# Moving the second norm of a hybrid backbone step from the token rows to the gathered expert rows

## The reference

```
h   = modulate(rmsnorm(x, norm_mix), sh1, sc1)
q, k, v, p = split(h @ w_in)
mix = concat(attention(q, k, v), pool_mixer(p)) @ w_out
x1  = x + g1 * mix
h2  = rmsnorm(x1, norm_ffn) * (1 + sc2) + sh2
affin = softmax(h2 @ w_router)            # 16 experts
gates, idx = top_k(affin.T, cap)          # 128 latent rows, 32 context rows per expert
y   = (silu(h2[idx] @ w_gate) * (h2[idx] @ w_up)) @ w_down * gates
out = rmsnorm(x1 + g2 * scatter_add(y, idx), norm_final)
```

## Time and profile before

| | us |
|---|---|
| median of 3 runs | 3756.24 (3752.21 to 3762.21) |
| profiled execution, device time | 3750.03 |
| its span in the trace | 3748.1 |

### The profile page before, as it was taken

How to read it: one execution, slowest core, us unless ns; L and a number is a source line. 1 busy time by engine, 2 the same in 40 slices (tenths; PEclk the granted TensorE clock), 3 DMA queues, 4 the chain that set the end, 5 groups by cost and what they waited for, 6 DMA issues and landing times.

```text
span 3748.1 us, 52148 instructions
## 1 busy us (share of the span) xinstructions
PE 3361.9 (90%) x20987; PEld 3033.8 (81%) x20987; DVE 2121.6 (57%) x2206; ACT 1786.9 (48%) x1933; POOL 524.7 (14%) x581
## 2 busy tenths in 40 slices
PE   5899999997889889996676999999999999999991
PEld 4677777776668777786566999999999999999991
DVE  4634433454543345324675777677767777777774
ACT  5643432554542246213324555555555555555552
POOL 1055045002220023002200000000000000000001
PEclk9999999998999889995787999999999999999995
DMA  7765555586133220522437888888888888888876
GB/s 251 259 225 190 180 186 184 185 287 217 35 135 135 90 77 29 202 101 87 166 107 256 274 262 258 256 271 274 274 268 268 265 273 264 257 255 271 274 240 249
DMA packets 541926, 781.11 MB, mean 208 GB/s; under 512 B 15680, under 2 KB 408944, under 8 KB 529408
## 3 DMA queue, kind: packets, MB, share of 16 engines
q1 hardware_dynamic: 507072, 616.60, 50.2%
q0 software_dynamic: 34752, 163.10, 13.2%
HBM read 713.51 MB, written 66.13 MB: 208 GB/s over the span
## 4 chain that ended last, share of the span: by engine, by line
PE 75%; DVE 9%; ACT 5%; DMA 4%; POOL 4%; issue 3%; ACTq 0%; POOLq 0%; DVEq 0%
PE PS L736 29%; PE PS L738 12%; PE PS L536 11%; PE PS L670 9%; DVE wlo L1070 2%; PE PS L628 2%; PE PS L694 2%; ACT whi L809 1%; PE PS L643 1%; PE PS L597 1%; DMA arena_ab<-k_rope 1%; PE PS L613 1%; PE PS L684 1%; PE PS L600 1%; DVE lo_f L1304 1%
## 5 line engine op out<-in xcount | busy, mean ns | idle before, releaser
L1304 DVE TENSOR_TENSOR lo_f<-raw_f,hi_f 128x2048 fp32r<-128x2048 f32 x384 | 878.4, 2291 | 390.9 <-ACT hi_f L999 390.3
L736 PE MATMUL PS<-xT,hi_f 128*128 128x320 f32 x4096 | 1055.7, 346 | 0.0
L738 PE MATMUL PS<-xT,lo_f 128*128 128x160 f32 x4096 | 966.2, 236 | 0.0
L1070 DVE TENSOR_TENSOR wlo<-raw,whi 128x2048 fp32r<-128x2048 f32 x204 | 472.1, 2333 | 552.3 <-ACT whi L809 551.8
L738 PEld LDWEIGHTS PS<-xT,lo_f 128*128 128x128 f32 x4096 | 782.8, 191 | 0.0
L736 PEld LDWEIGHTS PS<-xT,hi_f 128*128 128x128 f32 x4096 | 769.2, 188 | 0.0
L999 ACT ACTIVATE hi_f<-raw_f 128x2048 fp32r<-128x2048 f32 x384 | 731.3, 1908 | 72.1 <-PE PS L738 63.0
L809 ACT ACTIVATE whi<-raw 128x2048 fp32r<-128x2048 f32 x204 | 386.5, 1916 | 471.0 <-PE PS L670 196.9
L736 PE MATMUL PS<-hid,hi_f 128*128 128x320 f32 x2048 | 533.6, 346 | 0.0
L738 PE MATMUL PS<-hid,lo_f 128*128 128x160 f32 x2048 | 482.8, 236 | 0.0
L738 PEld LDWEIGHTS PS<-hid,lo_f 128*128 128x128 f32 x2048 | 390.8, 191 | 0.0
(11 more groups left out here) (247 smaller groups left out, 4705.4 us busy)
## 6 DMA issues: line engine op xcount, KB each, us to landing
raw_f<-w_gate SPq DMA_DIRECT2D x128, 1024.0 KB, 6.7
raw_f<-w_up SPq DMA_DIRECT2D x128, 1024.0 KB, 5.7
raw_f<-w_down SPq DMA_DIRECT2D x128, 1024.0 KB, 5.5
raw<-w_ada SPq DMA_DIRECT2D x96, 1024.0 KB, 5.2
raw<-w_in SPq DMA_DIRECT2D x60, 1024.0 KB, 5.3
raw<-w_out SPq DMA_DIRECT2D x48, 1024.0 KB, 5.1
arena_cd<-mod_rows POOLq DMA_DIRECT2D x9, 1024.0 KB, 8.4
arena_ab<-x_sample POOLq DMA_DIRECT2D x8, 1024.0 KB, 9.3
```

The source lines that it names most:

```text
L736: nc.tensor.matmul(PS[:, b + m, 0:2 * CAP], hi_f[:, n % NSPL_F, r, w], x, start=(kt == 0), stop=False, skip_group_check=True)
L738: ins = nc.tensor.matmul(PS[:, b + m, 0:CAP], lo_f[:, n % NSPL_F, r, w], x[:, 0:CAP], start=False, stop=(kt == last_kt), skip_group_check= ...
L1070: nc.vector.tensor_tensor(wlo[:, n % NSPLIT], raw[:, n % NRAW], whi[:, n % NSPLIT].bitcast(F32), ALU.subtract).then_inc(lo_ok, 1)
L1304: nc.vector.tensor_tensor(lo_f[:, n % NSPL_F], raw_f[:, n % NRAW_F], hi_f[:, n % NSPL_F].bitcast(F32), ALU.subtract).then_inc(f_lo_ok, 1)
```

## The change

Three things change together.

1. **The norm goes to the gathered rows.** The router product is taken of plain `x1` with `w_router` scaled by `(1+sc2)*norm_ffn` (`wra`), the logits are multiplied by rstd and the product `sh2 @ w_router` (`cb`) is added. `x1` and 8 copies of rstd are stored as rows of `h_s`, `h_q`. GpSimd gathers them and applies rstd, table and shift to 128 rows of 2048 and to 128 rows of 512 (the 32 context rows in quarters), before every expert (`modulate`).
2. **`x1` is streamed** in slices of 512 columns with two buffers; transposes and router products of a slice stand between the pieces of the next column group. In exchange the output projection has two weight slots in place of three, and its first two pieces are split inside the attention. Queries, keys and the first mixer of the next chunk are fetched during the output projection.
3. **`PE_PAD`** goes from 143 to 64 and `w_router` is loaded later, after the front.

```diff
-NRAW = 3 ... PE_PAD = 143
+NRAW = 3, NSPLIT = 3, NOUT = 2, EXT = 8 ... PE_PAD = 64
@@ tensor
+            def turn_x1(u):
+                for m in range(nt):
+                    pe.wait_ge(x1_ok, x1_by(tc, cc) - nt + m + 1)
+                    for r in range(4):
+                        last = nc.tensor.transpose(PS[:, 4 * (cc % 2) + m, r * P:(r + 1) * P], x1b[u % 2][:, m, ...], ident[:])
+                    last.then_inc(h2_tr, 1)
+            def route(u):
+                for m in range(nt):
+                    pe.wait_ge(h2T_ok, x1_by(tc, cc) - nt + m + 1)
+                    for r in range(4):
+                        last = nc.tensor.matmul(PS[:, 4 * (cc % 2) + m, 0:NE], h2T[:, m, r, :], wra[:, cond, 4 * cc + r, :], ...)
+                    last.then_inc(h2T_used, 1)
+            pe.wait_ge(mod_in, 9 * 16)
+            nc.tensor.transpose(PS[:, 7, 0:5 * KT], modr, ident[0:5 * KT, 0:5 * KT]).then_inc(mod_tr, 1)
+            pe.wait_ge(col2_ok, 1)
+            for c in range(2):
+                for kt in range(KT):
+                    last = nc.tensor.matmul(PS[:, 6, c * NE:(c + 1) * NE], s2col[:, c, kt:kt + 1].to_broadcast([P, P]), wr[:, kt, :], ...)
@@ tensor, output projection
                     for kg in range(4):
+                        if cc and kg == 2:
+                            turn_x1(u - 1)
+                        if cc and kg == 3:
+                            route(u - 1)
                         hi, lo = next_piece()
@@ tensor, experts
-                        pe.wait_ge(gs_in, e * 16 + 32)
-                        pe.wait_ge(gp_in, e * 16 + 32)
+                        pe.wait_ge(h_in, e + 2)
@@ scalar and vector, attention
+                    if k in (unit_end[tc] - 2, unit_end[tc] - 1):
+                        split_hi()      # vector: split_lo()
@@ vector, after the output projection of a chunk
-                nc.vector.scalar_tensor_tensor(out=tabA2, in0=tabA2, scalar=1.0, in1=nffn, op0=ALU.add, op1=ALU.mult)
-                residual(3)
-                for i in range(t0, t0 + nt):
-                    link(nc.vector.scalar_tensor_tensor(out=x, in0=x, scalar=rs2[:, 2, i:i + 1], in1=tabA2, ...))
-                    nc.vector.tensor_tensor(x, x, tabS2, ALU.add).then_inc(h2_ok, 1)
+                add_logits(4 * tc + 2)
+                residual(4 * tc + 3)
@@ gpsimd
+            for z in range(4):
+                dma(modr[z * KT:(z + 1) * KT, :], mod_d[z % 2, ...]).then_inc(mod_in, 16)
+            dma(modr[4 * KT:5 * KT, :], t["norm_ffn"]...).then_inc(mod_in, 16)
+            for z in range(4):
+                dma(wr[:, 4 * z:4 * z + 4, :], t["w_router"]...).then_inc(mod_in, 16)
+                if tc < 2:
+                    load_keys(tc + 1)
+                    load_q(t0 + nt)
+                    mixer(tc + 1, 0)
+                else:
+                    expert_tables()
+            def modulate(n, mid):
+                pool.wait_ge(gs_in, n)
+                pool.wait_ge(gp_in, n)
+                nc.gpsimd.tensor_scalar(g_s[:, 0:D], g_s[:, 0:D], g_s[:, D:D + 1], None, ALU.mult)
+                nc.gpsimd.tensor_scalar(g_p[:, 0:DQ], g_p[:, 0:DQ], g_p[:, DQ:DQ + 1], None, ALU.mult).then_inc(h_mid, 1)
+                pool.wait_ge(h_mid, mid - 1)
+                nc.gpsimd.tensor_tensor(g_s[:, 0:D], g_s[:, 0:D], a2_s[:], ALU.mult)
+                nc.gpsimd.tensor_tensor(g_p[:, 0:DQ], g_p[:, 0:DQ], a2_p[:], ALU.mult).then_inc(h_mid, 1)
+                pool.wait_ge(h_mid, mid)
+                nc.gpsimd.tensor_tensor(g_s[:, 0:D], g_s[:, 0:D], s2_s[:], ALU.add)
+                nc.gpsimd.tensor_tensor(g_p[:, 0:DQ], g_p[:, 0:DQ], s2_p[:], ALU.add).then_inc(h_in, 1)
             gather()
+            modulate(16, 2)
             with pool.Fori(0, NE) as e:
                 gather()
+                modulate(e * 16 + 32, e * 2 + 4)
```

More of the change, by code:

```diff
@@ L223, in hybrid_backbone_step @@
         pscale = keep("pscale", [P, PW // P])
-        wr = keep("wr", [P, KT, NE])
+        wra = keep("wra", [P, 2, KT, NE])
+        cb = keep("cb", [P, 2, NE])
         nmc = keep("nmc", [P, KT])
@@ L422, in x1_by, with outs_by, slot, raw_by @@
             return sum(4 * CH[c][1] for c in range(tc)) + (cc + 1) * CH[tc][1]
+        def outs_by(u):
+            return sum(CH[v // 4][1] - 1 for v in range(u + 1))
+        def slot(n):
+            return n % NRAW if n < D0 else (n - D0) % NOUT
+        def raw_by(n):
+            return sum(1 for v in range(n + 1) if slot(v) == slot(n))
+        def turn_at(tc):
+            return unit_start[tc] + (2 if CH[tc][2] == 0 else 1)
+        def route_at(tc):
+            return turn_at(tc) + 2
         def k_turned(tc, kt):
@@ L665, in _ @@
                             kt = kg * KG + r
-                            for m in range(nt):
-                                s = slice(m * P, (m + 1) * P)
-                                for z, (w, x) in enumerate(((ahi[:, kt, s], hi[:, r, :]), (alo[:, kt, s], hi[:, r, :]),
-                                                            (ahi[:, kt, s], lo[:, r, :]))):
-                                    last = nc.tensor.matmul(PS[:, 4 * (cc % 2) + m, :], w, x,
-                                                            start=(kt == 0 and z == 0), stop=(kt == KT - 1 and z == 2))
@@ L699, in _ @@
-            pe.wait_ge(aff_ok, TT)
+                            s = slice(m * P, (m + 1) * P)
+                            for z, (w, x) in enumerate(((ahi[:, kt, s], hi[:, r, :]), (alo[:, kt, s], hi[:, r, :]),
+                                                        (ahi[:, kt, s], lo[:, r, :]))):
+                                last = nc.tensor.matmul(PS[:, 4 * (cc % 2) + m, :], w, x,
+                                                        start=(kt == 0 and z == 0), stop=(kt == KT - 1 and z == 2))
@@ L700, in _ @@
+                            if kt == KT - 1 and m < nt - 1:
+                                last.then_inc(out_ok, 1)
+                        last.then_inc(used, 1)
+            turn_x1(11)
+            route(11)
+            pe.wait_ge(aff_ok, 3)
             for i in range(ST, TT):
[L701 removed]
+                last = nc.tensor.transpose(PS[0:NE, 6, (i - ST) * P:(i - ST + 1) * P], aff[:, i, :], ident[:])
@@ L1411, in _ @@
             dma(pscale[:], t["pool_scale"]).then_inc(consts_in, 16)
-            for z in range(4):
-                dma(wr[:, 4 * z:4 * z + 4, :],
-                    t["w_router"][0, z * 512:(z + 1) * 512].rearrange("(t p) e -> p t e", p=P)).then_inc(consts_in, 16)
             def bias_row(n):
```

474 lines of the change are left out of this document (295 added, 179 removed).

## The result

Three executions of the changed kernel took 3818.11, 3831.76 and 3848.51 us, median 3831.76 (a fourth, disturbed, took 11237.1 us and is left out here; with it the median is 3840.14). The kernel before took 3754.34 beside it (3752.21 to 3762.21). The ratio is 1.0205, 95% interval 1.0151 to 1.0259: the change makes the kernel slower, by about 2%. The profiled execution is the fastest of the three, 3818.1 us, 68.1 more than that of before.

A forecast was written before the change was run, and what follows sets the result against it. TensorE was taken to bound the expert loop and latent projections, VectorE the context projection, waits the seams. -71 before the experts and +107 in them gave +36, 3792 us; own range 3765 to 3830, wider range 3715 to 3855.

The forecast's parts named there:

- rival 3: Expert loop: GpSimd dearer, TensorE's clock down after stalls; 9 to 12 us an expert, about 3850; chance 0.18.
- Experts: Expert loop: GpSimd and VectorE take turns, TensorE stalls 6.7 us an expert, +107 for 16; sign 110 to 111 us each.
- VectorE gains back at most 5 us a round: Expert loop: VectorE's idle time, about 5 us per round of four pieces, makes good its delay.
- Seams: Between output projection and next attention: waits of 55.6 and 54.9 us go, moved work stays; -31 and about -30.
- Early split: Start of output projections: TensorE's 4.9 us wait falls away, 3 of it kept for each of two chunks, -6.
- First attention: Before the first keys: nine small loads, `wra` and 32 products with `w_router` delay them; +14, from 8 to 18.
- The start: Kernel start: fewer empty instructions and later `w_router` bring TensorE's first product to about 13 us; -9.8, or -6.
- Context chunk: Context output projection: VectorE loses work, but GpSimd's tables and the slices' transposes and products hold it up; +2.
- Behind it: From context projection to first expert: shorter chain through context top-k, then 15.5 us of uncovered `modulate`; -10.
- Rival 1: Expert loop: slack swallows the lock, 2 to 3.5 us an expert, about 3730; chance 0.17.
- Rival 2: Expert loop: no lock between GpSimd and VectorE for these operations, nothing lost, 3685; chance 0.05.
- Rival 4: Seams: small operations in the next attention's first units stall engines, each gives only 20; 3812; within the forecast's 0.55.

The follow-up runs named there:

- e1: The changed kernel with the six arithmetic operations of `modulate` left out, its waits kept: 3692.01 us, ratio 0.9807 to the kernel before.
- e4b: The kernel before with `PE_PAD` = 64 and 79 empty instructions put where TensorE waits for the top-k: 3763.97 us, ratio 1.0001.
- e4_pad: The kernel before with `PE_PAD` = 64 in place of 143 and nothing else: 3926.86 us, ratio 1.0445.
- e9: The changed kernel with the second norm on VectorE and the router's constant by VectorE sums and one product: 3873.14 us, ratio 1.0296 to the kernel before.
- e11: The changed kernel with `modulate` in 512-column slices, early gather, one product for the router's constant, 124 empty instructions at the top-k: 3764.85 us, ratio 1.0014.

## Why the prediction was right where it was, and wrong where not

The direction was right: slower, because the experts lose more than the front gains. So was the cause of the largest term, shown by e1. The time measured is 40 us above the forecast by the median of the three (48 by the median of all four) and 32 by the profiled executions. That is inside the range of 3715 to 3855, but just past the end of the forecast's own range, 3830, and nearer to rival 3's 3850 than to 3792. Of the 32, 24 are the front and 9 the experts.

- **Experts, 107 forecast, 116 measured** (111.3 us an expert, its sign was 110 to 111). The stall before down was forecast at 3.6 to 4 us and is 3.9. The 2.4 us at the fourth gate hardly exist (0.3). In their place stands the half clock behind the stall, 3.1 us, which the prediction had left to the upper end. The sum came out near because one missed term took the place of a wrong one, which is luck. The step that was wrong is "VectorE gains back at most 5 us a round": it counted idle time as usable, and the ring gives back 1.43. GpSimd's work was sized at 15.2 us alone and is 18.5, nearly all of it the scaling (5.45 + 1.56 against 2.7 + 0.8).
- **Seams, -31 and -30 forecast.** They vanished as forecast, and TensorE is full through the projections. The work in the next attention was sized right (10.4 us for 9.8). The mis-sized term is the three slices of a projection, 14.4 us: 20.9 in the first and 15.5 in the second. 15.5 is their own time, at a granted clock of 0.99; the 5.4 more are half clock, 3 us of it behind the block shown (the profiles of the other kernels with the same blocks have one level or the other).
- **Early split, -6 forecast.** In the profile the first attention grew by 2.4. Its splits (`whi` and `wlo`, 1.9 and 2.3 us, twice) stand in the chain behind the last heads; what TensorE no longer waits at the projection's start, it waits ahead of it. The note in the forecast that they stand in front of the last head was right, its price was not.
- **First attention, +14 forecast, about +17 measured.** The products cost 13.84 us for 12.2, the rest are the loads and VectorE's `wra`.
- **The start, -9.8 forecast.** -8.8 in the profile, but in e4b and in the mean of nine profiles nothing of it is left at 900 us. It can't be counted as a gain of the change.
- **Context chunk.** Attention and projection together grew by 15.4 us where some 12 were forecast.
- **Behind it, -10 forecast, -8.5 measured**, by another chain: the stores `h_q` (10.23 and 3.64 us) and the rstd columns in front of the gather, not top-k. Right by size, wrong in what it runs through.

Rival 1 (slack swallows the lock) falls with the ring: there is no slack of 5 us a round. Rival 2 (no lock) falls with the rows of an expert. Both conditions of rival 3 came true: the scaling costs even more than a two-input operation (18.5 us of GpSimd work an expert, where the rival set in at 18), and the clock falls behind the stalls. Its price did not: 7.2 us an expert where it had 9 to 12. The total came near its 3850 because the part ahead of the experts gained 47 us in place of 71. Rival 4's price, 10 us a seam, is close to what the first seam missed (9.5 with its half of the early split); the second and the context projection together missed 4. And its cause is another: the loss is in the projections, not in the first units of the attention.

## What to carry to other kernels

Before idle time of an engine is counted as room for new work, look at what ends that idle time: if it is an engine that in turn waits for this one, time the ring of both when it is late, and only the difference to the bottleneck's pace is room. Here work that had to take turns with another engine cost by its longest instruction, so cut it into slices no longer than what stands behind it can bear (2% slower became 0.7% faster here). And if a change moves code ahead of a long loop, look at the instruction queue's packets before anything else is compared.

## What the runs showed that was not expected

- TensorE's loop loaded its code again for every turn in two kernels whose loop had moved by 79 or 124 instructions: 206 packets in place of 71, 172 us in e4_pad and 125 in e9. The change under study keeps `PE_PAD` and the other edits in balance: in the compiled program its loop starts one instruction from where it was. With another count the comparison could have been of something else. The padding that keeps the loop in place is not free where TensorE is waited for: 3.9 us in e4b, 11 in e11.
- A stall of 3.9 us was followed by half clock, 3.1 us an expert; one of 1.5 us cost 0.3 on top of itself (29.4 less 23.9, by 16). Half clock also followed 29 of 54 blocks of 32 narrow product instructions, without any stall, and none of the groups of 8.
- GpSimd: 128x2048 with one input and a scale per partition 5.45 us, with two inputs 4.49.
- Profiles of kernels alike up to that point reach the first attention within 22 us of each other, which is more than several terms that one wanted to measure there. Such terms can be read from one profile's chain only, not from totals.
